# The first gate of a recurrence multiplied in high and low parts

## What is computed

```python
D_RNN, N_RNN_HEADS, RNN_HEAD_DIM = 1536, 16, 96
v = causal_depthwise_conv(xb, conv_b_w, conv_b_b)       # width 4
r = sigmoid(block_diag_linear(v, w_a, b_a))             # first gate
i = sigmoid(block_diag_linear(v, w_x, b_x))             # second gate
log_a = -8.0 * r * softplus(-lam)
a, mult = exp(log_a), sqrt(-expm1(2.0 * log_a))         # mult = 1 at token 0
h_t = a_t * h_{t-1} + mult_t * i_t * v_t                # scan over the tokens
y_b = (h * gelu(gb)) @ w_b_out
```

## Time and profile before

| | us |
|---|---|
| median of three executions | 2432.29 |
| the profiled execution | 2432.7 |
| its span | 2430.5 |
| TensorE busy (matmuls) | 2408.6 |
| VectorE busy | 1405.3 |
| ScalarE busy | 820.1 |
| span of the gate matmuls | 103.0 to 629.7 |

### The profile page before, as it was taken

How to read it: one execution, slowest core, us unless ns; L and a number is a source line. 1 busy time by engine, 2 the same in 40 slices (tenths; PEclk the granted TensorE clock), 3 DMA queues, 4 the chain that set the end, 5 groups by cost and what they waited for, 6 DMA issues and landing times.

```text
span 2430.5 us, 26081 instructions
## 1 busy us (share of the span) xinstructions
PE 2408.6 (99%) x10904; PEld 1956.1 (80%) x10904; DVE 1405.3 (58%) x1952; ACT 820.1 (34%) x1232; POOL 2.2 (0%) x7
## 2 busy tenths in 40 slices
PE   8999999999999999999999999999999999999999
PEld 6778688687788888888888888888878877888888
DVE  8799599698779734443233232234557544462377
ACT  5552442433513713332032131133333133122364
POOL 0000000000000000000000000000000000000000
PEclk9999999999999999999999999999999999999999
DMA  4202112012131112311111111112211111211232
GB/s 137 57 22 57 57 35 74 27 44 74 35 104 44 44 52 74 92 52 47 49 47 50 52 44 52 44 52 63 78 46 55 44 36 44 57 53 48 70 85 81
DMA packets 225406, 138.38 MB, mean 57 GB/s; under 512 B 13057, under 2 KB 216193, under 8 KB 225289
## 3 DMA queue, kind: packets, MB, share of 16 engines
q1 hardware_dynamic: 225288, 136.72, 19.2%
HBM read 127.75 MB, written 8.95 MB: 56 GB/s over the span
## 4 chain that ended last, share of the span: by engine, by line
PE 91%; DVE 4%; ACT 4%; issue 1%; DMA 0%; SPq 0%; DVEq 0%; ACTq 0%
PE bank L609 28%; PE bank L610 28%; PE bank L611 28%; PE bank L679 2%; PE bank L1015 1%; PE bank L920 1%; DVE uw L2338 0%; PE bank L902 0%; ACT whi L1053 0%; ACT bank L1156 0%; DVE uc L2065 0%; ACT lru L1159 0%; PE bank L949 0%; DVE wlo L1691 0%; PE bank L967 0%
## 5 line engine op out<-in xcount | busy, mean ns | idle before, releaser
L609 PE MATMUL bank<-h_hi,whi 128*128 128x512 f32 x1984 | 780.7, 393 | 10.0 <-DVE wlo L1691 10.0
L611 PE MATMUL bank<-h_hi,wlo 128*128 128x512 f32 x1984 | 773.1, 390 | 0.0
L610 PE MATMUL bank<-h_lo,whi 128*128 128x512 f32 x1984 | 773.0, 390 | 0.0
L609 PEld LDWEIGHTS bank<-h_hi,whi 128*128 128x128 f32 x1984 | 373.0, 188 | 92.0 <-issue 11.7
L610 PEld LDWEIGHTS bank<-h_lo,whi 128*128 128x128 f32 x1984 | 373.1, 188 | 79.5 <-issue 2.9
L611 PEld LDWEIGHTS bank<-h_hi,wlo 128*128 128x128 f32 x1984 | 372.9, 188 | 78.2
L1053 ACT ACTIVATE whi<-raw 128x1024 fp32r<-128x1024 f32 (+1 forms) x211 | 215.2, 1023 | 452.0 <-PE bank L611 417.3
L1691 DVE TENSOR_TENSOR wlo<-raw,whi 128x1024 fp32r<-128x1024 f32 (+1 forms) x211 | 249.5, 1185 | 163.6 <-ACT whi L1053 162.4
L609 PE MATMUL bank<-ff_hi,whi 128*128 128x512 f32 x512 | 199.6, 390 | 0.0
L610 PE MATMUL bank<-ff_lo,whi 128*128 128x512 f32 x512 | 199.2, 389 | 0.0
L611 PE MATMUL bank<-ff_hi,wlo 128*128 128x512 f32 x512 | 199.2, 389 | 0.0
(11 more groups left out here) (372 smaller groups left out, 3100.4 us busy)
## 6 DMA issues: line engine op xcount, KB each, us to landing
raw<-in_w_in SPq DMA_DIRECT2D x92, 512.0 KB, 3.7
raw<-in_w SPq DMA_DIRECT2D x64, 512.0 KB, 4.0
raw<-in_w_b_out SPq DMA_DIRECT2D x16, 384.0 KB, 3.1
raw<-in_w_out SPq DMA_DIRECT2D x11, 512.0 KB, 3.4
x_in<-in_x_t SPq DMA_DIRECT2D x8, 512.0 KB, 7.1
raw<-in_w_a_out SPq DMA_DIRECT2D x8, 512.0 KB, 3.9
raw<-in_w_o SPq DMA_DIRECT2D x8, 512.0 KB, 4.1
xcols<-in_x_t SPq DMA_DIRECT2D x16, 256.0 KB, 3.0
```

The source lines that it names most:

```text
L609: pe.matmul(target, lh, rh, start=start, stop=False, skip_group_check=True)
L610: pe.matmul(target, lh, rl, start=False, stop=False, skip_group_check=True)
L611: last = pe.matmul(target, ll, rh, start=False, stop=stop and point is not None, skip_group_check=True)
```

## The change

The first gate's products become split products. Every group therefore splits its three tiles of v and its first gate's weights ahead of the gates (`gate_inputs`). The parts of v take the place of `vg`, the low part of the weights takes the place of the weights, and the high part takes a place among the constants, where `ident`, `ones_sq` and `mask` lie later. So those are loaded or set after the last group, copies for the start (`ident_x`, `ones_x`) lie where v comes later, the halved parameters are cut to the 144 that are used, and POOL clears the first gate's buffer for each group again. The output of tile c can be split only when v[c] has been read by all first gates, so the split moves into `gated(g, c)`: for tiles 0 and 2 at the end of `gate_tile` as before, for tile 1 just ahead of `gate_tile(g, 2)`, which for g < 3 is behind `xb_tile(g + 1, 0)` and no longer before it.

```diff
@@ constants
-        parh = sb("parh", "const", 2048, [P, ROWS])
+        parh = sb("parh", "const", 2048, [P, HALVED])
...
+        gate_hi = sb("gate_hi", "const", 3680, [P, 7, P], F32R)
+        ident = sb("ident", "const", 3680, [P, P])
+        ones_sq = sb("ones_sq", "const", 4192, [P, P])
...
+        gate_lo = sb("gate_lo", "g", o, [P, len(PAIRS), P], F32R); o += 2 * 3584
@@ SP: load_gates
-                    w.wait_ge(*at("gate_w_clear", n))
+                    w.wait_ge(*at("gate_w_clear", 0, g) if not n else at("gate_w_clear", 1))
@@ SP: before the reloads of uc
+            sp.dma_start(ident[:], A["ident"]).then_inc(*landed("ident", ("ident",)))
+            sp.dma_start(mask[:], A["mask"]).then_inc(*landed("mask", ("mask",)))
@@ TensorE: gate_tile
-                    w.wait_ge(*at("gate_w", g, n))
+                    w.wait_ge(*(at("gate_w", g, n) if n else at("gate_lo", g)))
...
+                            if n == 0:
+                                w.wait_ge(*at("v_lo", g, a))
+                                i = PAIRS.index((a, c))
+                                three_products(b[:], (gate_hi[:, i, :], gate_lo[:, i, :]), (vg[0][a][:, cut(half)], vg[1][a][:, cut(half)]),
+                                               m == 0, [("gate", g, c, 0, half)] if m == len(rows_) - 1 else None)
+                                continue
@@ ScalarE
-                w.wait_ge(*at("lru", j))
+                if c != 1:
+                    gated(g, c)
+
+
+            def gated(g, c):
+                w.wait_ge(*at("lru", g * GT + c))
+                w.wait_ge(*at("gate", g, min(c + 1, GT - 1), 0, 1))
+                split_hi((f"vg{g}_hi", c), vg[0][c][:], T1[:])
+
+            def gate_inputs(g):
+                for t in range(GT):
+                    w.wait_ge(*at("rnn_in", g, t))
+                    if g:
+                        w.wait_ge(*at("yb", g - 1, 3, 1, 1))
+                    split_hi(("v_hi", g, t), vg[0][t][:], v[t][:])
+                w.wait_ge(*at("gate_w", g, 0))
                 if g:
-                    w.wait_ge(*at("yb", g - 1, 3, 1, 1))
-                split_hi((f"vg{g}_hi", c), vg[0][c][:], T1[:])
+                    w.wait_ge(*at("gate", g - 1, GT - 1, 0, 1))
+                split_hi(("gate_hi", g), gate_hi[:], gate_w[0][:])
@@ ScalarE and VectorE: the order of a group
                 for t in range(1 if g else 2, GT):
                     gb_tile(g, t)
+                gate_inputs(g)
...
                     xb_tile(g + 1, 0)
+                    gated(g, 1)
                     gate_tile(g, 2)
@@ VectorE
+            def gated(g, c):
                 w.wait_ge(*at(f"vg{g}_hi", c))
                 split_lo((f"vg{g}_lo", c, 0), vg[1][c][:], T1[:], vg[0][c][:], (f"vg{g}_lo", c, 1))
+
+            def gate_inputs(g):
+                for t in range(GT):
+                    w.wait_ge(*at("v_hi", g, t))
+                    split_lo(("v_lo", g, t), vg[1][t][:], v[t][:], vg[0][t][:])
+                w.wait_ge(*at("gate_hi", g))
+                split_lo(("gate_lo", g), gate_lo[:], gate_w[0][:], gate_hi[:])
@@ VectorE: after the groups
+            w.wait_ge(*at("gate", NG - 1, GT - 1, 0, 1))
+            dve.memset(ones_sq[:], 1.0).then_inc(*did(("ones_sq",)))
@@ POOL
+            for g in range(1, NG):
+                w.wait_ge(*at("gate", g - 1, GT - 1, 0, 1))
+                pool.memset(gate_w[0][:], 0.0).then_inc(*up("pool_done", ("gate_w_clear", 0, g)))
```

More of the change, by code:

```diff
@@ L146, in build_program @@
         par = sb("par", "const", 0, [P, ROWS])
-        parh = sb("parh", "const", 2048, [P, ROWS])
[L148 to L161, removed]
+        parh = sb("parh", "const", 2048, [P, HALVED])
+        ones = sb("ones", "const", 2624, [P, 8])
+        sp4 = sb("sp4", "const", 2656, [P, 16])
+        nsp4 = sb("nsp4", "const", 2720, [P, 16])
+        stat = sb("stat", "const", 2784, [P, 32])
+        small = sb("small", "const", 2912, [P, 192])
+        gate_hi = sb("gate_hi", "const", 3680, [P, 7, P], F32R)
+        ident = sb("ident", "const", 3680, [P, P])
+        ones_sq = sb("ones_sq", "const", 4192, [P, P])
+        xcol = sb("xcol", "const", 4704, [P, 32])
+        mprev = sb("mprev", "const", 4832, [P, 32])
+        wcol = sb("wcol", "const", 4960, [P, 32])
+        acol = sb("acol", "const", 5088, [P, 32])
+        gcol = sb("gcol", "const", 5216, [P, 16])
+        rcnt = sb("rcnt", "const", 5280, [P, 64])
+        mask = sb("mask", "const", 5536, [P, P])
         offsets, row = {}, 0
@@ L422, in build_program @@
         landings = (["par", "gain_in"] + [f"x{half}_{j}" for half in range(2) for j in range(0, DT, 2)] + ["raw0", "raw1"]
-                    + ["ident", "mask", "gate0", "gate1", "xc0", "xc1", "mem", "gates", "bias", "rcnt", "row_out", "mp", "last", "gain"]
+                    + ["ident", "ident_x", "mask", "gate0", "gate1", "xc0", "xc1", "mem", "gates", "bias", "rcnt", "row_out", "mp", "last", "gain"]
                     + [f"{n}{i}" for n in ("mb", "nb") for i in range(2)] + [f"sz_in{p}" for p in range(NP)]
@@ L637, in spread @@
                 b = b or bank(name, half)
+                unit = ident_x if name == "x_scale" else ident
+                w.wait_ge(*at("ident_x" if name == "x_scale" else "ident"))
                 for q in range(4):
                     t = half * 4 + q
-                    last = pe.matmul(b[:, q * P:(q + 1) * P], stat[:, column + t:column + t + 1].broadcast_to([P, P]), ident[:],
+                    last = pe.matmul(b[:, q * P:(q + 1) * P], stat[:, column + t:column + t + 1].broadcast_to([P, P]), unit[:],
                                      start=True, stop=True)
@@ L680, in gate_tile @@
                                              stop=m == len(rows_) - 1)
-                        last.then_inc(*up("pe_done", ("gate", g, c, n, half)))
+                        if n:
+                            last.then_inc(*up("pe_done", ("gate", g, c, n, half)))
             def conv_blocks(j):
@@ L727, in mean_sum @@
                 w.wait_ge(*at("uc_total", DT - 1, half))
+                w.wait_ge(*at("ones_sq"))
                 w.wait_ge(*at("free", *sum_users[half]))
@@ L780, in turn_memory @@
                 b = bank("mem", j)
+                w.wait_ge(*at("ident"))
                 w.wait_ge(*at("mem_normed", 0))
@@ L1717, in vector @@
             dve.memset(ones[:], 1.0).then_inc(*did())
-            dve.memset(ones_sq[:], 1.0).then_inc(*did(("ones",)))
+            dve.memset(ones_x[:], 1.0).then_inc(*did(("ones",)))
             dve.memset(xb_in[:, 0:PAD_B], 0.0).then_inc(*did(("xb_pad",)))
```

26 lines of the change are left out of this document (15 added, 11 removed).

## The result

The changed kernel takes 2451.41 us (median of four executions, 2450.79 to 2451.52) against 2432.31 for the kernel before, measured beside it: a ratio of 1.0075 with an interval of 1.0064 to 1.0087, or +19.1 us. The forecast was 2456.5 with a range of 2445 to 2468. The direction and the places were right, the size 5 us too high. The profiled execution has a span of 2449.5 us against 2430.5, so the two traces together hold 19.0 us to be explained.

The account below looks back on a forecast made before the run. TensorE, busy 2408.6 of 2430.5 us, was taken as the bound. Groups 0 to 3 cost 7.2 + 2.7 + 2.7 + 9.05, plus 2.5 for the clock: +24.2 us, giving 2456.5 against the median, range 2445 to 2468.

Parts of the forecast that it names:

- The saving: First gate, all groups: each product falls from 0.859 to 0.698 us, saving 0.161, in all 9.0 us.
- three passes: First gate's products: by the skill's four-pass rule alone they would cost 0.644 us each, the gain 12.0 us.
- The waits for the splits: TensorE waits before the first gate: 4.8 us in group 0, 11.3 in group 3, none in groups 1 and 2.
- The chain: Groups 0 to 2: tile 1's later split delays tile 2's line 1829, 8.90 us behind; groups 1 and 2 end 2.7 later.
- the second-gate wait: Tile 2's second gate in groups 0 to 2: TensorE waits 2.6 us instead of 0.8.
- the wait at `xb(g+1, 1)`: Bank of `xb(g+1, 1)`, groups 0 to 2: freed late by line 1829 of tile 2, a new wait of 3.4 us.
- The clock: TensorE falls to half rate behind group 3's 11.3 us wait, costing 2.5 us; nothing behind waits of 2.6 to 4.8.
- The rival that had a fall at each wait: Clock also falls behind the 4.8 us wait and three 3.4 us waits: +10 us, 2466.5; chance 0.14.
- The bank wait hidden: Rival for groups 0 to 2: tile 2's chain is not late; +14.0 us in all, 2446.3; chance 0.13.
- T0: Start of a group's gate matmuls on TensorE; forecast at 107.85 us in group 0.
- The faster rival: First gate, all groups: 0.161 us saved per product with all splits under cover, -9.0 us, 2423.3; chance 0.03.
- The small edits: Constants loaded late and POOL's memsets: taken together at nothing, with a bound of 0 to +2 us.

Follow-up runs that it names:

- the wait made early: The kernel before, with ScalarE waiting for the next tile's first gate ahead of the split of the output: 2429.66 us.
- the wait made again: The changed kernel, with ScalarE waiting once more on the already satisfied first gate ahead of its first tanh of tiles 1 and 2: 2459.34 us.
- the fillers: The changed kernel, with useless matmuls (18 in group 0, 44 in group 3) filling TensorE's two waits for the low part of the gate weights: 2447.04 us.
- the second experiment: The changed kernel, with tile 1's output split ahead of `xb_tile(g + 1, 0)` again in groups 0 to 2: 2444.68 us.
- both orders mended: The changed kernel, with the gate inputs split earlier and tile 1's output split ahead of `xb_tile(g + 1, 0)` again: 2431.79 us.
- the pair with 0.15 us: The changed kernel with inputs split earlier and tile 1's output split ahead of `xb_tile`: split products 2431.79 us, plain fp32 first gate 2431.94.
- the pair with 4.25 us: The changed kernel with both splits moved ahead and tile 2's gates one block later: split products 2427.23 us, plain fp32 first gate 2431.48.
- the two versions with early splits: The changed kernel, gate inputs split ahead of the gelus (group 0: decay constants): 2438.09 us; also with tile 1's output split ahead of `xb_tile`: 2431.79.
- third gate later: The changed kernel, both splits moved ahead, tile 2's gates one block later in groups 0 to 2: 2427.23 us; with plain fp32 first gate 2431.48.
- the three with one cost taken out: The changed kernel with group 3's first gate in fp32 (2440.15 us), tile 1's output split ahead of `xb_tile` (2444.68), or useless matmuls filling two waits (2447.04).
- the first fp32 version: The changed kernel, both splits moved ahead, first gate in plain fp32 of the weights' low part alone (wrong result, timing only): 2431.94 us.

## Why the prediction was right or wrong

**The saving: right.** 0.161 per product was forecast, 0.859 - 0.69 = 0.17 measured in group 1. The 0.644 for three passes, which would have given 3.0 us more, wasn't borne out: the matmuls start 0.231 apart, nearly as the `yb` rows had them.

**The waits for the splits: right.** 4.8 and 11.3 were forecast, TensorE was idle 4.75 and 10.99, and undoing group 3 alone gave back 11.2, against the forecast's 9.05 + 2.5. The reading that the splits of groups 1 and 2 hide behind two conv blocks was right too: 277.19 has no idle time before it.

**The chain: right mechanism, one term mis-sized.** "From such a difference to line 1829 of the next tile it takes 8.90" was carried over unchanged; it measured 7.57, twice in each of groups 0 to 2. I had the table load in the sum, and had `gated`'s new wait in the diff, and didn't ask what that wait does to the instruction behind it. With 1.33 less, the second-gate wait is 2.6 - 1.33 = 1.3 (measured 1.1), the wait at `xb(g+1, 1)` is 3.4 - 1.33 = 2.0 from start to start (measured 2.0, 1.7 of it idle), and a group ends 2.7 - 2 x 1.33 = 0 later (measured 0.0). That is 8.0 us of the forecast. Both directions were shown: the wait made early takes 3.75 us from the kernel before, the wait made again adds 7 to the changed one and brings back the forecast's own waits, 2.42 and some 3.1.

**The clock: half right.** "The others (2.6 to 4.8) are nearer to 1.1 than to 9.6: nothing" failed at 4.75: it cost 2.5 there, and 2.5 at 10.99 as forecast. The waits at `xb(g+1, 1)` came out at 1.7 and left the clock up. The rival that had a fall at each wait was thus right for group 0; its falls behind waits of 3.4 were not put to the test, since no such wait arose. What it says of the 2.6 us waits, that a fall there would vanish in the next one, is what the kernel with the wait made again shows behind 2.42. The Trainium skill ("TensorE: Matmul & The Clock Gate", What's actually happening), which the prediction names beside that rival, has the array throttled unless activity releases it; the fillers, which kept the clock at 1.00 through both waits, agree.

**The bank wait hidden:** this rival was wrong about the wait, which came in all three groups, and the second experiment shows that the order made it. Its number, 2446.3, was as far from the result (5.1) as the forecast's.

**Not foreseen:** the fall near 1785 (+1.2), and that the gates of group 0 start at 106.99 and not at 107.85. Most of that is TensorE's first matmul, 0.7 us earlier (8.91 against 9.60 in the earlier trace rows). It lies between 8.6 and 9.5 in the other profiles (9.16 in the kernel before with the wait made early), so it is no effect that can be put down to the change.

**Sum.** 24.2 - 8.0 (chain) + 2.5 (clock in group 0) + 1.2 (clock at 1785) - 0.9 (an earlier T0) = 19.0, as measured. The errors partly cancelled: without the clock's two falls and the early T0 the forecast would have been 8 us out. The result lies below 2452 to 2461, the band that the forecast gave itself, and it is this cancelling that brings it so near.

**The faster rival** was priced at 2423.3 with the splits under cover. The nearest real version, with both orders mended, took 2431.79 and gained nothing that shows. Cover for the splits wasn't enough, since the tensor program's gain was waiting time from then on. The small edits (constants loaded late, POOL's three memsets of 2.5 us in all) cost nothing that the traces show.

## What to carry to other kernels

Taking work from the engine that is busy 99% of the time pays only as far as the chain that crosses it can keep up; measure that by putting the slower instruction back with everything else in place, as the pair with 0.15 us and the pair with 4.25 us between them did. When a change adds or moves a wait, look at the instruction behind it too, since a wait that was already satisfied was worth 7 us here by where it stood. Splits needed by the next stage belong ahead of the work that only that stage's end needs: moving them and one order line turned +19 us into -1.3, that is, into no difference from before. The last group got 11.0 us of that; group 0, where VectorE has no slack, only 2.6.

## What the runs showed of the hardware

**A table load runs beside a wait, or behind it.** With one wait left for the activation that needs the table, the load of 1.28 us ran first and beside VectorE's 1.14 us difference. With two, it began when the difference had landed. The chain differs by 1.33 us. That it is the number of waits on the activation, and not another property of the program around it, rests on four kernels (before, after, and each with one wait added) and on no measurement of a wait by itself. In the other eight profiles, all with the wait made early, no load ahead of this tanh waits for `vg_lo`. Whether the order of the two waits would do in place of their number wasn't tried.

**More than the length of a pause decides whether the clock falls.** The table has idle times of TensorE and how the matmuls behind them ran. Extra time is what they took beyond the same matmuls at full clock.

| idle before | where | clock | extra us |
|---|---|---|---|
| 10.99 | gates of group 3, changed kernel | fell | 2.5 |
| 10.99 | the same, wait made again | fell | 1.6 |
| 4.75, 4.19 | gates of group 0, changed kernel and wait made again | fell | 2.5, 1.7 |
| 4.07, 3.54 | the two versions with early splits, group 0 | fell | 1.7, 1.5 |
| 2.55 | early splits, 606.38 | stayed | |
| 2.52 | third gate later, 594.67 | fell | 1.4 |
| 2.42 | the wait made again, 141.67 and the same place in groups 1 and 2 | fell | 1.7 each |
| 1.7, 1.1 | the changed kernel, three each | stayed | |

Two pauses of the same 2.5 us went different ways. A pause of half a microsecond can be enough too. Between 1760 and 1795 every version stands idle for 0.26 us and, in all but one, again for 0.28 to 0.46 a microsecond later. The clock fell there in eight of the twelve profiles: the changed kernel, the three with one cost taken out, the two with early splits and both with the third gate later. It stayed up in the kernel before, in the same with the wait made early, in the changed kernel with the wait made again and in the first fp32 version. From the last `yb` to the end of the span the four without the fall take 1723.8 to 1723.9 us and the eight with it 1724.9 to 1725.9, so that this fall costs 1.0 to 2.0. What tells these apart stays open; none of the runs varied it alone.
